# Two-layer hybrid trunk: first weight section in quarters, small loads later, more readerless matmuls, expert units 0 and 1 in halves

## The reference, cut to what matters

```
u = rms_norm(x, norm_mix_g[l]) @ w_in[l]              # 1024 x 3328
aq, ak, av, bq, bf, bi, bg, cb, cc, cx = split(u)
o_a = differential_attention(aq, ak, av, positions, ...)   # partial rotary, q/k norm
o_b = hgrn2(bq, bf, bi, bg, lower_bounds[l], ...)          # gated linear recurrence
o_c = short_conv(cb, cc, cx, conv_w[l])
x = x + concat(o_a, o_b, o_c) @ w_out[l]
h = rms_norm(x, norm_ffn_g[l])
# router: top group of 4, in it the top 2 of 8 experts; 32 experts in all
y[t] = sum over t's two experts e of gate(t, e) * (silu(h[t] @ w_gate[e]) * (h[t] @ w_up[e])) @ w_down[e]
x = x + y
```

## Time and profile before

| | before |
|---|---|
| median of 3 runs | 1205.41 us (1204.53 to 1205.55) |
| the profiled execution | 1204.86 us |
| its span, first to last instruction | 1203.1 us |
| busy PE / VectorE / ScalarE / GpSimd | 881.2 / 505.6 / 171.3 / 36.9 us |
| read from memory | 440.30 MB, 367 GB/s over the span |
| mean granted clock of PE | 0.89 of full |

### The profile page before, as it was taken

How to read it: one execution, slowest core, us unless ns; L and a number is a source line. 1 busy time by engine, 2 the same in 40 slices (tenths; PEclk the granted TensorE clock), 3 DMA queues, 4 the chain that set the end, 5 groups by cost and what they waited for, 6 DMA issues and landing times.

```text
span 1203.1 us, 19819 instructions
## 1 busy us (share of the span) xinstructions
PE 881.2 (73%) x8249; PEld 522.8 (43%) x8249; DVE 505.6 (42%) x1307; ACT 171.3 (14%) x479; POOL 36.9 (3%) x75
## 2 busy tenths in 40 slices
PE   6999987665757575755799999776757575667557
PEld 4576564342424242423465675543324232333244
DVE  3766565332423242423457674642424242424233
ACT  2334221100000000000113442100000000000000
POOL 2001100000000000000000120000000000000000
PEclk9999999887978897977999999897889788878878
DMA  8936559999999999999997173799999999999996
GB/s 271 364 166 221 199 218 430 426 427 428 427 429 428 428 428 429 430 427 426 417 387 295 71 278 132 287 428 427 427 428 428 428 429 427 429 429 429 428 424 273
DMA packets 54603, 442.20 MB, mean 368 GB/s; under 512 B 9216, under 2 KB 12304, under 8 KB 29200
## 3 DMA queue, kind: packets, MB, share of 16 engines
q1 hardware_dynamic: 54544, 441.36, 88.5%
HBM read 440.30 MB, written 1.05 MB: 367 GB/s over the span
## 4 chain that ended last, share of the span: by engine, by line
PE 55%; DMA 33%; DVE 8%; issue 2%; SPq 1%; ACT 0%; DVEq 0%
DMA ring<-in_expert_w_up 29%; PE psum L779 15%; PE psum L814 9%; PE psum L823 6%; PE psum L794 6%; PE psum L691 5%; PE psum L898 5%; PE psum L764 4%; DMA work<-in_expert_w_down 2%; DVE work L1415 2%; PE psum L846 1%; DVE work L1426 1%; DMA maps<-in_expert_w_down 1%; DMA ring<-in_expert_w_gate 1%; DVE work L1421 1%
## 5 line engine op out<-in xcount | busy, mean ns | idle before, releaser
L779 PE MATMUL psum<-ring,work 128*32 128x256 f32 x3968 | 270.0, 433 | 105.5 <-DMA ring<-in_expert_w_up 99.3
L779 PEld LDWEIGHTS psum<-ring,work 128*32 128x32 f32 x3968 | 150.0, 125 | 227.8 <-issue 165.6
L794 PE MATMUL psum<-ring,work 128*32 128x256 f32 x1664 | 142.8, 502 | 129.8 <-DVE work L1421 125.7
L1413 DVE TENSOR_SCALAR work<-work 128x128 f32<-128x128 f32 x62 | 14.0, 227 | 324.0 <-ACT work L1087 324.0
L794 PEld LDWEIGHTS psum<-ring,work 128*32 128x32 f32 x1664 | 61.6, 135 | 199.5 <-DVE work L1421 148.7
L814 PE MATMUL psum<-ring,hT 128*128 128x512 f32 x256 | 113.4, 600 | 5.3 <-DVE hT L1471 5.2
L1426 DVE COPY work<-psum 32x256 f32<-32x256 f32 x124 | 52.6, 424 | 153.4 <-PE psum L794 152.3
L691 PE MATMUL psum<-work,h 128*128 128x128 f32 x512 | 70.9, 304 | 39.0 <-DVE work L1379 30.1
L691 PEld LDWEIGHTS psum<-work,h 128*128 128x128 f32 x512 | 67.7, 217 | 50.9 <-DVE work L1379 36.9
L1091 ACT ACTIVATE work<-psum 32x256 f32<-32x256 f32 x124 | 46.2, 373 | 283.9 <-PE psum L794 283.2
L814 PEld LDWEIGHTS psum<-ring,hT 128*128 128x128 f32 x256 | 48.6, 193 | 63.5 <-issue 57.3
(11 more groups left out here) (283 smaller groups left out, 705.9 us busy)
## 6 DMA issues: line engine op xcount, KB each, us to landing
ring<-in_expert_w_gate SPq DMA_DIRECT2D x64, 2048.0 KB, 18.5
ring<-in_expert_w_up SPq DMA_DIRECT2D x62, 2048.0 KB, 22.8
ring<-in_expert_w_down SPq DMA_DIRECT2D x52, 2048.0 KB, 23.7
ring<-in_w_in SPq DMA_DIRECT2D x12, 2048.0 KB, 18.6
work<-in_expert_w_down SPq DMA_DIRECT2D x6, 2048.0 KB, 20.9
ring<-in_w_out SPq DMA_DIRECT2D x4, 2048.0 KB, 8.8
maps<-in_expert_w_down SPq DMA_DIRECT2D x2, 2048.0 KB, 9.6
ring<-in_expert_w_up SPq DMA_DIRECT2D x4, 1024.0 KB, 23.9
```

The source lines that it names most:

```text
L779: last = T.matmul(bank[GU_BANK[i % 2]][CAP * j:CAP * j + CAP, 0:2 * P], xg[:, k, CAP * i:CAP * i + CAP], gate_up[:, :, k, P * j:P * j + P] ...
L794: last = T.matmul(bank[5][CAP * q:CAP * q + CAP, 0:2 * P], actT[i % 2][:, CAP * j:CAP * j + CAP], down[j][:, 2 * P * q:2 * P * q + 2 * P], ...
```

## The change

1. **Loads.** Section 0 is loaded in four pieces of two k-tiles, each with its own semaphore; x's second tile goes between the second and the third piece (in layer 1 there are only the four pieces). Positions and the two `prow` loads go behind section 1, the other parameter loads behind section 2.
2. **PE at the start of a layer.** Tile 0 of x is transposed; `aq0` begins with the first quarter of `hT` and the first piece of the section; tile 1 is transposed in the midst of `aq0`. The transpose of `prow` goes behind `bq`. At the start of the program eight matmuls on `ones` run that nothing reads.
3. **VectorE and ScalarE.** `mixer_norm` comes first and moves tile 1 into `hT` only after `diag`; `rotations` and `lower_bounds` follow, `parameters` goes behind `hgrn_inputs`. ScalarE copies the row norms before sine, cosine and the exponential.
4. **Router.** Four readerless matmuls instead of three behind the logits, and two more behind the counts.
5. **Turn 0.** Units 0 and 1 run all gate matmuls, then all up matmuls, each of 128 columns; the end of a gate half releases the slot of its weights (`gate_read`), and three loads are issued on these releases. The gate transposes follow unit 1, on ScalarE too.

```diff
@@ sync: loads
+            def first_section(l):
+                ...
+                for n in range(4):
+                    part = slice(2 * n, 2 * n + 2)
+                    if n == 2 and l == 0:
+                        e.dma_start(x[:, 1, :], rows_of[1]).then_inc(x_in[1].sem, 16)
+                    e.dma_start(tiles[:, part, :], w_in[:, part, :]).then_inc((early_part[n] if n < 3 else ring_full[s]).sem, 16)
             e.dma_start(x[:, 0, :], rows_of[0]).then_inc(x_in[0].sem, 16)
-            e.dma_start(x[:, 1, :], rows_of[1]).then_inc(x_in[1].sem, 16)
             e.dma_start(gmix[:, :, :], by_feature("norm_mix_g")).then_inc(gain_in.sem, 16)
+            first_section(0)
+            mixer_section(0, 1)
             e.dma_start(pos_i[:, :], a["positions"][0].rearrange("(i p) -> p i", p=P),
                         allow_slow_non_contiguous=True).then_inc(pos_in.sem, 16)
-            mixer_section(0, 0)
...
-            mixer_section(0, 1)
+            mixer_section(0, 2)
...
-            mixer_section(0, 2)
             e.dma_start(gffn[:, :, :], by_feature("norm_ffn_g")).then_inc(router_in.sem, 16)
...
+                e.wait_ge(gate_read.sem, gate_read.after(l, 1))
+                part(ring_full, four[0], 4, 0)
+                e.wait_ge(gate_read.sem, gate_read.after(l, 2))
+                part(ring_full, place(l, FIRST[3][0]), 3, 0)
                 e.wait_ge(main.gu_ps.sem, main.gu_ps.after(first, 1))
-                part(ring_full, four[0], 4, 0)
-                e.wait_ge(main.gu_ps.sem, main.gu_ps.after(first, 2))
-                part(ring_full, place(l, FIRST[3][0]), 3, 0)
                 part(ring_full, four[1], 4, 1)
@@ tensor
+            e.wait_ge(const_ok.sem, ONES_MADE)
+            for n in range(WARM_UP):
+                T.matmul(bank[7][:, 0:P], ones[:, :], ones[:, :], start=True, stop=True)
             e.wait_ge(const_ok.sem, IDENT_MADE)
...
+                if order is OVERLAPPED:
+                    expert_units(S, turn, order[0:2], slots, loaded, True)
+                    gate_transposes(S, turn)
+                    expert_units(S, turn, order[2:], slots, loaded, True)
...
+                        if first_group and i < 2:
+                            for part in range(2):
+                                for k in range(KT):
+                                    if i == 0 and part == 0 and k % 4 == 0:
+                                        e.wait_ge(S.xg_ok.sem, S.xg_ok.after(turn, 1 + k // 4))
+                                    for j in range(4):
+                                        last = T.matmul(bank[GU_BANK[i]][CAP * j:CAP * j + CAP, P * part:P * part + P],
+                                                        xg[:, k, CAP * i:CAP * i + CAP], gate_up[:, part, k, P * j:P * j + P],
+                                                        start=(k == 0), stop=(k == KT - 1))
+                                last.then_inc(S.gu_ps.sem if part else gate_read.sem, 1)
+                            continue
...
+                e.wait_ge(ht_sb.sem, ht_sb.after(l, 1))
+                for k in range(KT):
+                    if k == KT // 2:
+                        e.wait_ge(ht_sb.sem, ht_sb.after(l, 2))
+                        stream_ready(e, l, 1)
+                        transposed_rows(1, x[:, 1, :].rearrange("p (c k) -> p k c", k=KT))
+                    if k == KT - 2:
+                        section(AQ)
+                    elif k % 2 == 0:
+                        e.wait_ge(early_part[k // 2].sem, early_part[k // 2].after(l, 16))
+                    last = T.matmul(bank[PROJ_BANK["aq0"]][:, :], hT[:, k, 0:P], Waq[:, k, :], start=(k == 0), stop=(k == KT - 1))
...
                 W = section(B)
+                e.wait_ge(ht_sb.sem, ht_sb.after(l, 4))
                 project_columns(W, "bq", 0)
+                if l == 0:
+                    e.wait_ge(rows_in.sem, 32)
+                    T.transpose(bank[0][:, 0:DEPTH * 8], prow, ident[0:DEPTH * 8, 0:DEPTH * 8]).then_inc(pro_pe.sem, 1)
...
-                for n in range(KEPT_WARM):
-                    T.matmul(bank[7][:, :], ident[:, :], masks[:, 0:4, :], start=True, stop=True)
+                keep_warm(4)
...
+                keep_warm(2)
@@ vector
+                mixer_norm()
                 if l == 0:
                     rotations()
-                mixer_norm()
-                if l == 0:
                     lower_bounds()
+                hgrn_inputs()
                 if l == 0:
                     parameters()
-                hgrn_inputs()
```

## The result

| | before | after |
|---|---|---|
| time, median (range) | 1205.48 us (1204.53 to 1208.19, 4 runs) | 1194.24 us (1193.13 to 1195.96, 4 runs) |
| profiled execution, its span | 1204.86 us, 1203.1 us | 1193.82 us, 1191.9 us |
| mean granted clock of TensorE, as a share of 2.4 GHz | 0.890 | 0.893 |

The account below looks back on a forecast made before the run. Two limits were taken: PE work end to end in the mixers, the DMA weight stream in the experts. 4.4 + 3.2 + 4.7 - 0.2 = 12.1 us off 1204.86 gave 1192.8 us, range 1190 to 1200.

Parts of the forecast that it names:

- part 2: Router to experts: kept clock and split units issue the first gate load 3.2 us earlier in layer 0, 4.7 in layer 1.
- part 1: Start of layer 0: `bq` starts 5.3 us earlier, less 0.2 and 0.7, so 4.4 us (2.1 to 5.9).
- (a): Router to experts: the readerless matmuls don't hold the clock at the gather; 1196.5 us, chance 0.18.
- (c): Units 0 and 1: the split halves don't run side by side, each release 5.7 us later; 1204.2 us, chance 0.02.
- (e): Another wait ahead of `bq` and a stream gone dry at the restart undo the gain; 1204 us, chance 0.02.
- (d): Mixers: more early PE work lets the clock fall inside a mixer; slower, up to 1241 us, chance 0.03.
- Part 1's term for section B: Start of layer 0: B lands at 17.2 us, 1.4 us earlier by moving small loads behind it; bounds 16.4 to 18.6.
- Rival (b): Start of layer 0: B lands no earlier and PE runs slowly after the gap; 1195.0 us, chance 0.14.
- The slow clock behind the gap: Before `bq` in layer 0: PE idle 1 to 2.5 us may then run slowly, 0 to 1.4 us lost, 0.7 taken.
- Dry stream: Experts' restart: SP's wait for unit 1's down might dry the weight stream; up to 0.7 us a layer, range only.
- Layer 1's start: From layer 1's transposes to `bq`: within 0.2 us of before, taken as 0.2 us of loss.
- The bytes are a fixed sum: Experts' stream: an earlier first load after the mixer comes off the end, unless the stream runs dry again.

Follow-up runs that it names:

- positions first: Against the kernel after: the positions load put back ahead of layer 0's first section; 1193.65 us in one run.
- one piece: Against the kernel after: layer 0's first section in one load, x's second tile ahead of it; 1197.67 us in one run.
- the kernel after, again: The changed kernel unaltered, measured once more; 1192.80 us, ratio 0.9899 to the kernel before.
- part 1 alone: Against the kernel before: only the start of the layers changed, router and turn 0 as before; 1203.03 us, ratio 0.9975.
- the kernel with the gate half ahead: Against the kernel with section B in halves: last turn's unit 2 computes its gate half before waiting for the up matrix; 1188.87 us, ratio 0.9859.

## Why the prediction was right, and where it missed

**The size** held: 12.1 us forecast, 11.2 and 12.7 in the two measurements, within the range. **The mechanism** held for part 2 (clock kept, halves side by side), which makes 8.1 of the 11.3 us in the table; for part 1 it held only in that `bq` starts when B lands, not in that B lands much earlier. The rivals (a), (c) and (e) are out: gathers of 3.81 us, split units of 7.19 us, and a time far below 1204. So is (d) at its price: the clock is 1.00 from 18.2 to 157 us and from 608.5 to 745. But the sign named for it did show, a clock of 0.51 for 3.4 us at the start of layer 1's mixer, worth 1 us (below). No wait of PE from `bq` to the gather of layer 0 was longer than 0.5 us.

**Part 1's term for section B** was mis-sized: 17.2 us taken, 18.22 measured, 16.7 again; `bq` at 18 or later was the prediction's own sign for it. The step that failed is "I take off 1.4 us" for the small loads now behind B. In six executions with the new order of loads `bq` waits for B until 16.71, 17.86, 17.93, 18.27, 18.41 and 18.61 us; 17.2 lies inside, but near the early end. With positions first it waits until 18.50, inside the scatter, and with the four pieces undone B still lands at 18.1. So most of the lead of `bq` is not B landing earlier (in the profiled executions 18.6 before and 18.2 after); it is that PE and VectorE are done by then, which they were not before. Rival (b) was right about the load in the first profile; its slow clock did not come there, but came in two other executions. The first median, 1194.24 us, lies nearer to its 1195.0 than to the forecast's 1192.8, the second, 1192.80, on the forecast: the time alone does not tell the two apart. The lower bound of part 1, 2.1 us, comes out as 2.3 from its own terms (22.54 - 18.6 - 0.2 - 1.4).

**The slow clock behind the gap**, taken as 0.7 of 0 to 1.4: of seven profiled executions in which `bq` waited 0.5 to 2.7 us, five paid nothing and two paid 1.7 us. None paid the mean that the sum took, though elsewhere costs between do occur (1.0 us at the start of layer 1, 1.4 in one piece). Here 2.59 us of idle PE cost nothing, so B's late landing (1.1 us) and the 0.7 us not paid stand against each other, and part 1 comes to 3.83 at the gather against 4.4. That they nearly cancel is luck.

**Part 2** was right in each term that counts: clock 1.46 us in layer 0 and 2.81 in layer 1 (forecast 1.4 and 2.8), the release and the later gate transposes the rest (1.92 in both). The 2.81 belongs to the one profiled execution of the kernel before, whose layer 1 gather took 6.62 us; in the two other traces without the added matmuls the gather took 5.44 in both layers, so what comes again is 1.6 us a layer. The 0.7 us for the split units was 0.08. The 31 ns came from a group of 64 in 1.96 us; 256 in one stream take 7.19, so 192 more cost 5.23 us or 27 ns each, and the rest, 0.2 us a group, is paid once and not four times.

**Dry stream**, up to 0.7 us for the range: it did not come. From 172 to 192 us the DMA engines move 418 to 434 GB/s in each stretch of 4 us; the first of them:

```profile
172.00:176.00 4.00, 4.00 (x103) 2.78 (x95) 3.46 (x8) 0.66 (x2) 0.00 (x0) 1.00 0.99 418
```

**Layer 1's start**, taken as a loss of 0.2: 1.34 measured. Some 1.0 of it is the clock at 0.51 from 598.0 to 601.4. In the kernel after, again, and in part 1 alone the same steps from the first transposes to `bq` took 10.03 us (596.85 to 606.88 in the first) against 11.08 here and 9.74 before, so the edit costs 0.3 and the rest is that execution's clock.

**"The bytes are a fixed sum"** is what the prediction got wrong in kind. It holds to the landing of the last turn's up matrix (7.75 us of lead after 7.21 at the restart). Behind it some twenty microseconds of work and short waits on PE stand against the last loads, and the two are close to balance: before, PE waits there 0.30 and 0.45 us for DMA; after, it does not, but works partly at half rate behind 9 us of idle time. In its trace part 1 alone lost all its lead there, and the whole change went from 7.75 to 6.78 us, 0.43 below its lead at the restart. In layer 1 the kernel before was the one that ran slowly (5.47 us behind 9.72 of idle time, then 2.48 and 3.18), and so the last step gave 1.09 us back: the misses of the two layers cancel in part, and that is luck too. The kernel with the gate half ahead bears this out in layer 0, where a shorter path on PE won 1.9 us with the up matrix landing as before; in layer 1 the loads left nothing to win.

## What to carry over

Two edits that each remove one of two things that end close together are costed together: alone they were worth 0 and 0.7 us here, both 4.3 (at full clock, by the estimate above, 0, 2 and 2.8). Where the next wait is a load whose landing scatters, cut that load so that its first part is enough; here it was worth 2 to 3 us and took the gap, and with it the scatter, out. And a stream's end is a stage of its own: read which wait ends last there before a lead from far ahead is carried through it.

## What the runs showed of the hardware

The granted clock behind idle time is not decided by the length of the gap alone: 2.59 us of idle PE were followed by 32 matmuls in 7.17 us, 2.66 us by the same in 8.86 and 2.16 us by 8.84. After gaps of 3.2 to 9.5 us in the last turn unit 2 took 4.9 to 6.6 us instead of 3.66 in both layers of every changed kernel that leaves unit 2 in one piece, and 5.47 us behind 9.72 in layer 1 of the kernel before, which in layer 0 had 3.66 behind 2.23 us. With the gate half ahead, each half took 3.6 us instead of 1.96 in three of four cases.

The column of the granted clock does not tell all at the start of a program: in the kernel before it stands at 1.00 from 13.3 to 22 us, but the first three records of `aq0` take 1.06 to 1.19 us and the last twelve 0.59, so there the durations have to be read.

The landing of section B, 2 MB behind the 3 MB of x and the first section, differs by 1.5 us between two executions of one kernel (16.7 and 18.2 us), and by 1.9 us between kernels that load in the same order up to there (16.7 to 18.6).
